# Moving the value loads of a decode attention stage from GpSimd's DMA queue to SyncE's, behind the key loads

## What is computed

```
for b in range(8):                        # one decode sequence at a time
    for (w, d) in ((128, 1), (512, 4), (2048, 16)):        # group A: three dilated windows
        idx = 2048 + arange(8)[:, None] - arange(w // d + 1)[None, :] * d
        kg, vg = take([cache_a_k ; new k], idx), take([cache_a_v ; new v], idx)
        s = (q . kg) * SCALE + bias;  p = exp(s - max(s));  o_i = (p / sum(p)) . vg
    o_a = the three o_i, mixed by their softmax denominators
    o_b = one window of 128 over cache_b_k, cache_b_v, times sigmoid(lse - sink)   # group B
```

## Time and profile before

| | |
|---|---|
| median of three runs | 2812.61 us (2811.31 to 2814.37) |
| the profiled execution | 2814.37 us, its span 2812.6 us |
| decode phase in the span | 865.8 to about 1008 us |
| TensorE busy | 93% of the span |
| mean granted TensorE clock | 0.968 |

### The profile page before, as it was taken

The page is one execution under the profiler, slowest core; times in us unless marked ns, Lnnn a source line. Parts: engine busy times, 40 slices in busy tenths (PEclk is TensorE's granted clock), DMA queues, the critical chain, the costliest instruction groups (busy, mean ns, idle before and its releaser), DMA issues.

```text
span 2812.6 us, 34922 instructions
## 1 busy us (share of the span) xinstructions
PE 2611.2 (93%) x13959; PEld 2255.9 (80%) x13959; DVE 697.4 (25%) x1648; ACT 985.6 (35%) x1685; POOL 1124.5 (40%) x677
## 2 busy tenths in 40 slices
PE   6999999789997948994999999999999999999997
PEld 4899999789995527773888887888878888988985
DVE  5421011066663235551101012010120101201102
ACT  4211221077774525552423324233242332421321
POOL 4200000057762312211645546455464564543641
PEclk8999999989998979997999999999999999999998
DMA  4311312199957946666444545445454464322222
GB/s 136 111 38 56 128 58 77 61 175 186 173 91 196 255 134 180 193 185 189 141 149 135 199 158 182 145 139 200 151 186 151 128 252 143 129 89 79 87 89 69
DMA packets 299831, 395.31 MB, mean 141 GB/s; under 512 B 81306, under 2 KB 233290, under 8 KB 295014
## 3 DMA queue, kind: packets, MB, share of 16 engines
q1 hardware_dynamic: 285968, 302.02, 38.1%
q10 hardware_dynamic: 7078, 70.34, 7.0%
q0 software_dynamic: 6624, 20.72, 2.7%
HBM read 327.68 MB, written 121.05 MB: 160 GB/s over the span
## 4 chain that ended last, share of the span: by engine, by line
PE 50%; DMA 2%; issue 1%; DVE 1%; ACT 0%; POOL 0%; SPq 0%; ACTq 0%; DVEq 0%
PE ml_y L1727 25%; PE ml_up L1698 8%; PE ml_up L1699 8%; PE ml_up L1700 8%; DMA ml_x<-scratch_x 1%; DMA ml_raw<-in_w_up 1%; PE ml_y L1722 1%; PE ml_y L1721 0%; DVE ml_a L1829 0%; DVE ml_y L1867 0%; DVE ml_y L1871 0%; ACT ml_square L1776 0%; POOL ml_w_lo L1659 0%; ACT ml_r L1756 0%; ACT ml_a_hi L1762 0%
## 5 line engine op out<-in xcount | busy, mean ns | idle before, releaser
L1659 POOL TENSOR_TENSOR ml_w_lo<-ml_raw,ml_w_hi 128x1024 fp32r<-128x1024 f32 x256 | 613.7, 2398 | 480.8 <-ACT ml_w_hi L1747 480.8
L1698 PE MATMUL ml_up<-ml_h_hi,ml_w_hi 128*128 128x512 f32 (+1 forms) x1280 | 453.1, 354 | 39.7 <-POOL ml_w_lo L1659 28.0
L1747 ACT CAST ml_w_hi<-ml_raw 128x1024 fp32r<-128x1024 f32 x256 | 268.1, 1048 | 589.4 <-PE ml_y L1727 401.6
L1700 PE MATMUL ml_up<-ml_h_hi,ml_w_lo 128*128 128x512 f32 (+1 forms) x1280 | 452.6, 354 | 0.0
L1699 PE MATMUL ml_up<-ml_h_lo,ml_w_hi 128*128 128x512 f32 (+1 forms) x1280 | 452.3, 353 | 0.0
L1727 PE MATMUL ml_y<-ml_w_hi,ml_a_hi 128*128 128x512 f32 x1024 | 398.5, 389 | 0.0
L1727 PE MATMUL ml_y<-ml_w_lo,ml_a_hi 128*128 128x512 f32 x1024 | 398.4, 389 | 0.0
L1727 PE MATMUL ml_y<-ml_w_hi,ml_a_lo 128*128 128x512 f32 x1024 | 398.3, 389 | 0.0
L1698 PEld LDWEIGHTS ml_up<-ml_h_hi,ml_w_hi 128*128 128x128 f32 x1280 | 242.4, 189 | 73.0 <-POOL ml_w_lo L1659 28.2
L386 PE MATMUL pj_acc<-pj_h_hi,pj_w_hi 128*128 128x424 f32 (+1 forms) x800 | 289.6, 362 | 1.0 <-DVE pj_h_lo L580 1.0
L387 PE MATMUL pj_acc<-pj_h_lo,pj_w_hi 128*128 128x424 f32 (+1 forms) x800 | 285.4, 357 | 0.0
(11 more groups left out here) (212 smaller groups left out, 3633.2 us busy)
## 6 DMA issues: line engine op xcount, KB each, us to landing
ml_raw<-in_w_up SPq DMA_DIRECT2D x64, 1024.0 KB
ml_raw<-in_w_down SPq DMA_DIRECT2D x64, 1024.0 KB
out_o_a_k_s<-in_cache_a_k ACTq DMA_DIRECT2D x8, 3060.0 KB, 12.2
out_o_a_v_s<-in_cache_a_v ACTq DMA_DIRECT2D x8, 3060.0 KB, 12.7
at_raw<-scratch_pt SPq DMA_DIRECT2D x36, 512.0 KB, 7.8
scratch_pt<-pj_proj SPq DMA_DIRECT2D x10, 1056.0 KB, 4.1
pj_w<-in_w_in SPq DMA_DIRECT2D x20, 512.0 KB, 3.9
op_part<-scratch_part SPq DMA_DIRECT2D x16, 594.0 KB, 6.3
```

Of the source, the lines that this page charges most:

```text
L1659: nc.gpsimd.tensor_tensor(split_of(w_lo, n), raw_of(n), f32(split_of(w_hi, n)), ALU.subtract).then_inc(w_lo_ready, 1)
L1698: pe.matmul(out, hi[:, k, :], h_hi[:, k, cols], start=(k == 0), stop=False)
L1700: last = pe.matmul(out, lo[:, k, :], h_hi[:, k, cols], start=False, stop=(k == DBLK - 1))
L1747: nc.scalar.copy(split_of(w_hi, n), raw_of(n)).then_inc(w_hi_ready, 1)
```

## The change

`load_values` moves from POOL's program to SP's. SP now waits for the four `zeroed` steps first, loads the values of sequence 0, and then alternates: keys b, values b, for b = 1 to 7. The waits inside `load_keys` and `load_values` are the same as before. POOL keeps its four memsets and issues no DMA in this phase. The ten DMAs of each set, their shapes and their semaphores are the same.

```diff
         @block.sync
         def _(sp):
 
+            def load_values(b):
+                s = b % 2
+                flat = d["cache_a_v"].rearrange("l b t h e -> (l b) t (h e)")[b]
+                new = d["kv"][SEQ:, :].rearrange("(b t) c -> b t c", t=DEC_T)[b]
+                if b >= 2:
+                    sp.wait_ge(weighed, 2 * (b - 1))
+                tiles = v[:, s, 0:KT * AW].rearrange("p (t c) -> p t c", c=AW)
+                for t in range(FAR_T):
+                    far = flat[t * 2 * P:(t + 1) * 2 * P, :].rearrange("(g r) c -> g r c", r=16)[:, 0:DEC_T, :]
+                    sp.dma_start(tiles[:, t, :], far).then_inc(v_in[s], 16)
+                sp.dma_start(tiles[:, FAR_T:, :], ...).then_inc(v_in[s], 16)
+                sp.dma_start(v[:, s, KT * AW:], ...).then_inc(v_in[s], 16)
+                sp.dma_start(v_new[0:DEC_T, s, 0:AW], ...).then_inc(v_new_in[s], 16)
+                sp.dma_start(v_new[DEC_T:2 * DEC_T, s, AW:], ...).then_inc(v_new_in[s], 16)
+
             def load_keys(b):
                 if b >= 2:
                     sp.wait_ge(kt_ready, NX * (b - 1))
                 load_decode_keys(sp, d, keep, b)
 
+            sp.wait_ge(zeroed, ZEROED)
+            load_values(0)
             for b in range(1, DEC_B):
                 load_keys(b)
+                load_values(b)
 
         @block.gpsimd
         def _(pool):
...
-            def load_values(b):
-                (the same, with pool for sp)
-
-            pool.wait_ge(zeroed, ZEROED)
-            for b in range(DEC_B):
-                load_values(b)
```

More of the change, by code:

```diff
@@ L2034, in _ @@
         def _(sp):
+            def load_values(b):
[8 more added lines that the diff above has]
+                    sp.dma_start(tiles[:, t, :], far).then_inc(v_in[s], 16)
+                sp.dma_start(tiles[:, FAR_T:, :], flat[PAST - NEAR:, :].rearrange("(t p) c -> p t c", p=P)).then_inc(v_in[s], 16)
+                sp.dma_start(v[:, s, KT * AW:], d["cache_b_v"].rearrange("l b t h e -> (l b) t (h e)")[b]).then_inc(v_in[s], 16)
+                sp.dma_start(v_new[0:DEC_T, s, 0:AW], new[:, AW:2 * AW]).then_inc(v_new_in[s], 16)
+                sp.dma_start(v_new[DEC_T:2 * DEC_T, s, AW:], new[:, 2 * AW + KVW:]).then_inc(v_new_in[s], 16)
             def load_keys(b):
```

## The result

The changed kernel takes 2836.97 us (median of 4 runs, 2832.76 to 2840.82) against 2813.49 us before. The ratio is 1.0082, with a 95% interval of 1.0065 to 1.0098. That is 18 to 28 us slower. I had forecast 2820.8 with a range up to 2826. The direction was right, the size was not.

What follows compares the result with a forecast made beforehand. TensorE, busy 93% of the span, was taken as the bound, with decode loads using nearly the whole DMA rate. Later period 7 (6.8 us) plus one clock fall (1.4) gave +8.2 us: 2820.8 from the median 2812.61, range 2813.5 to 2826.

Steps and rivals of the forecast that it cites:

- waits at periods 3, 5, 7: Decode phase: TensorE waits for late keys at every second set, 2.4, 2.1 and 2.1 us.
- waits at periods 4, 6: Decode phase: TensorE also waits a little for keys at these periods, 0.3 us each.
- the wait at period 7 of before, gone: Period 7 of the kernel before included a 1.18 us wait of its own, counted off the loss.
- removing POOL's issues at 0: Decode phase: nobody waited for POOL's ten DMA issues per period, so removing them is worth 0.
- The mechanism: SP's queue: keys b+1 stand behind the wait of values b, 17.4 us against 14.9; every second set pays.
- The rate of 269 GB/s: Rate taken for q1 alone in the decode phase: 15.2 us for a pair, 7.6 for a set.
- The aside that at 275 to 279 GB/s the result would be about 1 us smaller: Decode loads: by the Trainium skill one queue keeps the rate, making the loss about 1 us smaller.
- the landing time: Decode phase: from a set's last packet to TensorE's start on those keys takes 0.9 us.
- the faster rival: Decode loads: not slower, one queue runs faster without POOL's software queue, -2.9 to +4 us; chance 0.25.
- The start: Decode start: keys 1 stand behind values 0, so period 1 starts at 885.8, 0.9 us later.
- The clock: TensorE's granted clock falls once behind the new waits, costing 1.4 us; bounds 0 and 4.5.
- The slower rival: Decode phase: one queue doesn't fill the engines, or the clock falls every time, +10 to +14 us; chance 0.25.

Runs made afterwards that it cites:

- e9: The changed kernel timed again, unaltered: 2833.11 us, ratio 1.0064 against the kernel before.
- e3: The kernel before with its two queues, only load_keys(b) also waits for weigh(b - 3), so keys are issued late: 2820.59 us, ratio 1.0027.
- e5: The changed kernel, but behind the wait for weigh(b - 2) SP issues keys b+1 first, then values b: 2822.66 us, ratio 1.0027.
- e1: All loads on SP's one queue, but keys issued early, in the order of time of the kernel before: 2816.34 us, ratio 1.0011.
- e2: The changed kernel with three value slots, so load_values(b) waits for weigh(b - 3): 2826.67 us, ratio 1.0048.
- e7: Against the kernel before, keys and values all issued from POOL on its one software queue, keys early: 2822.38 us, ratio 1.0019.
- e10: The kernel before timed again, unaltered, as control: 2816.96 us, ratio 1.0006.
- e12: The kernel before, two queues, but POOL issues values 1 only once keys 2 have landed: 2818.01 us, ratio 1.0012.
- e11: The changed kernel with 24 unread transposes on TensorE ahead of the wait for keys 3, 5 and 7: 2833.88 us, ratio 1.0062.
- e4: The changed kernel with load_keys(1) put ahead of the wait for zeroed: 2830.33 us, ratio 1.0062.
- e8: The kernel before with keys 1 loaded a phase ahead, in the prompt attention phase: 2823.5 us, ratio 1.0035.

## Why the prediction was right in kind and too small

In order of the prediction's steps, by the length of the decode phase in the profiles of the change and of e9 (+22.6 and +18.8 us against 143.0):

| term | forecast | after | e9 |
|---|---|---|---|
| start of period 1 | +0.9 | +3.3 | +3.2 |
| period 1, part at half clock | 0 | -0.6 | -0.4 |
| waits at periods 3, 5, 7 | +6.6 | +15.8 | +9.9 |
| waits at periods 4, 6 | +0.6 | 0 | 0 |
| the wait at period 7 of before, gone | -1.2 | -1.2 | -1.2 |
| periods 3, 5, 7 at a lower clock | +1.4 | +5.0 | +6.0 |
| rest | 0 | +0.3 | +1.3 |

*What bounds the kernel, and removing POOL's issues at 0*: right. TensorE's periods without a wait and at the full clock are 14.9 us with POOL idle too.

*The mechanism* (keys b+1 behind the wait of values b; every second set pays; SP's own issue time hidden): right. e3 shows it by itself: lateness alone, with two queues, costs 7.6 us with waits at 3, 5 and 7. e5 shows that the place behind the values matters. SP's issue was done 2.3 us ahead of `weigh`'s end, where I had allowed 3.6. That TensorE would also wait a little at periods 4 and 6 did not come.

*The rate of 269 GB/s*: right for a pair from an empty queue (266 to 269 after), wrong as a property of the queue. Over a long stretch one queue carries 242 to 246 (e1, e2) or 239 (e7) and two carry 275 to 280 (before, e10). My four rows of q1 alone were short stretches between stretches of q0, and I rounded their mean of 265 upwards to 269 without a reason. The row at 232, which I gave to the slow rival, was the better hint. The aside that at 275 to 279 GB/s the result would be about 1 us smaller is a little low: the same steps give 1.2 to 2 us.

*The step that failed most is the landing time.* By the table, the change's profile is 14.4 us over the forecast and e9's 10.6. The start and the waits, which both hang on when keys land, are 11.0 and 5.0 of that, the clock 3.6 and 4.6. I took 0.9 us from the last packet to TensorE's start, from the earlier trace rows, where the queue was draining, and a mean rate for a set. But TensorE waits for a set's last step: keys 5 of the change had theirs at 966.76, 5.1 us behind the ninetieth per cent, and period 5 began at 966.80. From the issue of values b to the start on keys b+1 I had 17.4 us. It took 18.5, 23.2 and 18.6 in the change, 17.9, 17.6 and 18.8 in e9, and 18.1, 17.2 and 16.9 in e3 with two queues. So one such wait was 6 us over mine, the others up to 1.4. The earlier trace rows had shown just such a tail, and I used it only as an argument for the faster rival: that the lag would go with POOL's queue. It did not: one queue of either kind has it in nearly every set while it is full.

*The start*: I had keys 1 landing 15.2 + 0.9 us behind first data. Period 1 began 22.2 to 25.0 us into the phase in the six runs whose SP program starts like the change's, against 19.1. The forecast was 20.0. The issue (2.5 us into the phase) and the first data (1.4 us after it, 873.9) were as forecast. The missing 2 to 5 us are in part the tail again, 1.2 to 4.2 us from the ninetieth per cent to the last step in these runs, and in part the rate: e9 had the shortest tail and 261 GB/s from 870.2 to 888.5. My reason for a small loss, that values 1 no longer share the engines ahead of keys 1, did not hold: e12 kept them back, and period 1 began no earlier.

*The clock*: I counted one fall and took the edge between 1.55 and 2.28 us of idle time as sharp. It fell behind all three waits and took 1.3 to 2.1 us each time, 2.75 once. There is no such edge in these runs. The clock fell behind 2.13 us in e3 (period 7 took 16.6 us) and stayed up behind 3.50 us in e2 (period 3 took 15.0). How far this term adds to the waits is open (e11).

*The slower rival*, with 250 GB/s or three falls, was the nearest: the three falls came, at 266 to 269 GB/s for a pair. I had it at 0.25 and at up to +14, and it still fell short, as its landing time was the same 0.9 us. With the tail of the earlier trace rows on top (some 9 us for one set) the range would have ended at about 2836, a microsecond under the first timing and 3 over the second.

The single parts do not add up neatly. By timings, one queue alone is +3 (e1), lateness alone +7.6 (e3), the start 1 to 7 (e4): 12 to 18 of the 18 to 23. By the lengths of the phase in the profiles they are 8.3, 11.2 and 2.8 to 6.6, together 22 to 26 against 19 to 23. So whether anything is left over can't be told. Why the last steps of a set trail, and why two queues carried more than one, stays open.

## What to carry to other kernels

A DMA issue is an instruction in its engine's order: before moving loads to another engine, write down for each wait which later issues stand behind it and when those are wanted. A transfer has landed when its slowest engine is done, so take landing times from semaphores at a busy time of the same stage, tails included, and not from bytes over a mean rate. Where a stage needs nearly all of the DMA rate, its time to spare is an account: early issue fills it, a slower queue empties it period by period, and a test of the first few periods shows nothing.

## What the runs showed of the hardware

- With rows of 1536 bytes and DMA share at 1.03 to 1.05, a single queue moved 242 and 246 GB/s (SP's) and 239 (POOL's) over 76 to 108 us. The same sets over two queues moved 275 and 280 over 60 us. With two queues and long tails (e8) it was 256 over 90 us. The Trainium skill ("DMA: Bandwidth & Descriptors", "Rules for kernel authors") says that spreading DMAs over several issuing engines doesn't help bandwidth. In these runs two queues carried 4 to 17% more than one.
- The same page of the Trainium skill ("DMA: Bandwidth & Descriptors", "Latency and other measured facts") has two usually slower engines, and its best guess ties them to the GpSimd path. Here the last steps of a set trailed by 3.3 to 7.4 us with SP's queue alone and no DMA from POOL in the phase (e1, e2). Whether those engines are the ones that trailed can't be seen in the trace.
- The granted clock fell to half behind idle times of 2.8 to 4.0 us in e9, but stayed at 1.00 behind 3.33 us of idle time in e11's period 3 and behind 3.50 us in e2's. So the last idle time alone does not decide it.
